# Modulation products of a two-block transformer kernel: summed along the row by GpSimd and VectorE instead of over partitions by TensorE

## What is computed

```python
s_c = jax.nn.silu(c)
s_cc = jax.nn.silu(c_ctx)[None]
...
ml = (s_c @ w_mod[i] + b_mod[i]).reshape(-1, 3, 3, D)
...
mc = (s_cc @ w_mod[i] + b_mod[i]).reshape(-1, 3, 3, D)
h = gated_residual(h, ml, 0, swiglu(ada_in(h, norm_g[i, 0], ml, 0), ffn_w_in[i, 0], ffn_w_out[i, 0]), 0.5)
```

## Time and profile before

| | |
|---|---|
| device time, median of 3 runs | 3246.8 us (3246.36 to 3249.54) |
| span of the profiled execution | 3230.1 us; no time of its own is shown for it beside the runs |
| PE busy | 3136.0 us (97% of the span) |
| PEld busy | 2660.2 us (82%) |
| DVE busy | 1724.8 us (53%) |
| ACT busy | 1270.9 us (39%) |
| POOL busy | 1950.4 us (60%), in 1285 instructions |
| DMA | 430.35 MB, mean 133 GB/s |

### The profile page before, as it was taken

One profiled execution on the slowest core, in us unless ns is written; L12 is line 12 of the kernel. 1 busy time (PEld: TensorE's weight loads), 2 busy tenths in 40 slices (PEclk: granted clock), 3 DMA queues, 4 the chain that ended last, 5 costly groups with the idle time before them and its releaser, 6 DMA issues.

```text
span 3230.1 us, 48616 instructions
## 1 busy us (share of the span) xinstructions
PE 3136.0 (97%) x18046; PEld 2660.2 (82%) x18046; DVE 1724.8 (53%) x2409; ACT 1270.9 (39%) x2132; POOL 1950.4 (60%) x1285
## 2 busy tenths in 40 slices
PE   7999899999999999999999999999999999999998
PEld 6677899976779998888887777888888888886898
DVE  5665776655668865443435465544435443436554
ACT  4445555343555643222232443322223222235443
POOL 6658477514994975677567658678875777603000
PEclk9999999999999999999999999999999999999999
DMA  5323455632335663333443223334433443332354
GB/s 195 111 92 105 138 189 194 204 105 95 112 117 168 215 210 121 122 126 122 134 130 117 85 85 108 119 129 130 136 125 110 133 138 125 123 119 76 131 182 156
DMA packets 120280, 430.35 MB, mean 133 GB/s; under 512 B 13857, under 2 KB 17185, under 8 KB 119729
## 3 DMA queue, kind: packets, MB, share of 16 engines
q1 hardware_dynamic: 93632, 335.24, 31.7%
q0 software_dynamic: 24576, 86.46, 8.4%
q10 hardware_dynamic: 1904, 6.36, 0.5%
HBM read 426.95 MB, written 8.85 MB: 135 GB/s over the span
## 4 chain that ended last, share of the span: by engine, by line
PE 86%; POOL 5%; DVE 3%; ACT 2%; DMA 2%; issue 2%; ACTq 0%; DVEq 0%; SPq 0%; POOLq 0%
PE ps L484 22%; PE ps L486 21%; PE ps L485 21%; PE ps L511 2%; PE ps L581 2%; PE ps L582 2%; PE ps L583 2%; POOL macc L402 2%; DMA raw<-in_panels 2%; POOL modraw L400 2%; POOL mprod L400 1%; PE ps L525 1%; PE ps L530 1%; PE ps L526 1%; PE ps L986 1%
## 5 line engine op out<-in xcount | busy, mean ns | idle before, releaser
L1642 DVE TENSOR_TENSOR wlo<-raw,whi 128x1024 fp32r<-128x1024 f32 x632 | 856.0, 1355 | 914.6 <-ACT whi L1078 889.5
L1078 ACT ACTIVATE whi<-raw 128x1024 fp32r<-128x1024 f32 x632 | 668.4, 1058 | 1417.2 <-PE ps L486 901.2
L484 PE MATMUL ps<-xhi,whi 128*128 128x512 f32 (+2 forms) x2792 | 949.3, 340 | 3.1 <-DVE wlo L1642 2.5
L486 PE MATMUL ps<-xhi,wlo 128*128 128x512 f32 (+2 forms) x2792 | 934.6, 335 | 0.0
L485 PE MATMUL ps<-xlo,whi 128*128 128x512 f32 (+2 forms) x2792 | 933.7, 334 | 0.0
L484 PEld LDWEIGHTS ps<-xhi,whi 128*128 128x128 f32 x2792 | 531.8, 190 | 70.8 <-issue 14.8
L485 PEld LDWEIGHTS ps<-xlo,whi 128*128 128x128 f32 x2792 | 531.8, 190 | 51.8 <-issue 1.9
L486 PEld LDWEIGHTS ps<-xhi,wlo 128*128 128x128 f32 x2792 | 531.4, 190 | 50.2
L400 POOL TENSOR_SCALAR modraw<-modraw,cs 128x512 f32<-128x512 f32 x288 | 552.1, 1917 | 27.6
L400 POOL TENSOR_SCALAR macc<-modraw,cs 128x512 f32<-128x512 f32 x36 | 70.5, 1958 | 745.2 <-PE ps L511 602.5
L400 POOL TENSOR_SCALAR mprod<-modraw,cs 128x512 f32<-128x512 f32 x252 | 445.8, 1769 | 19.0 <-POOL macc L402 0.2
(11 more groups left out here) (362 smaller groups left out, 4752.9 us busy)
## 6 DMA issues: line engine op xcount, KB each, us to landing
raw<-in_panels SPq DMA_DIRECT2D x632, 512.0 KB, 3.3
modraw<-in_mod POOLq DMA_DIRECT2D x144, 512.0 KB, 4.4
bias_by_column<-in_rpb POOLq DMA_DIRECT2D x16, 476.2 KB, 8.3
bia<-bias_by_column POOLq DMA_DIRECT2D x32, 96.0 KB, 2.6
rtab<-in_rtab ACTq DMA_DIRECT2D x2, 1312.0 KB, 7.4
wuq<-in_wuq ACTq DMA_DIRECT2D x2, 768.0 KB, 6.7
con<-in_con SPq DMA_DIRECT2D x1, 1345.5 KB, 13.7
h<-in_x SPq DMA_DIRECT2D x1, 1088.0 KB, 6.7
```

Source lines behind the costliest of these rows:

```text
L484: pe.matmul(out, w_hi, x_hi, start=start, stop=False)
L486: return pe.matmul(out, w_lo, x_hi, start=False, stop=stop)
L1078: act.activation(whi[:, s * PW:(s + 1) * PW], raw[:, s * PW:(s + 1) * PW], ACT.Copy).then_inc(hi_split, 1)
L1642: dve.tensor_tensor(wlo[:, s * PW:(s + 1) * PW], raw[:, s * PW:(s + 1) * PW], whi[:, s * PW:(s + 1) * PW].bitcast(F32), ALU.subtract).then ...
```

## The change

POOL now gets the weights turned: the 128 outputs of a tile lie on the partitions and the 1024 inputs along the row, in two pieces of 512 (`MOD_W`), 256 KB each. The conditions are loaded once by SP as a row that is repeated on all partitions (`cb`, 128 x 2048), and ACT applies the silu to all of it after the first norm, where before it did so to 16 columns inside that norm. For each piece POOL multiplies by both conditions and then halves the row again and again by adding its second half to its first, for both conditions in one instruction, down to 32 columns (`MOD_FOLD`), which go to `modacc`. A group has 4 tiles of 2 pieces and so 4 x (6 + 7) = 52 instructions, all `tensor_tensor`, and 8 loads. The wait for `mod_done` moves from the group's start to its first write of `modacc`, the sixth instruction. PE's 36 groups of matmuls go, with the PSUM bank they took. DVE's `mod_tiles` waits for POOL itself, sums `modacc` (128 x 8 x 32) to 128 x 8 with a `tensor_reduce`, and then adds the bias. In the five norms it stands at the end instead of behind the diagonals. The places of all other groups on DVE stay.

```diff
-MS = 30
+MOD_W, MOD_FOLD = 512, 32
+
+
+MOD_OPS = (6, 7)
+MS = 4 * sum(MOD_OPS)
...
+            sp.dma_start(cb[:, :], t["cond"].broadcast_to([P, 2 * D])).then_inc(cond_in, 16)
...
-                acc = [macc[:, s * 512:(s + 1) * 512] for s in range(2)]
-                for q in range(4):
-                    s = q % 2
-                    w = [modraw[:, s * PW + k * 512:s * PW + (k + 1) * 512] for k in range(2)]
...
-                    for k in range(2):
-                        if q or k:
-                            step(mprod[:, :], w[k], c[0][k], ALU.mult)
-                            step(acc[0], acc[0], mprod[:, :], ALU.add)
...
-                    for k in range(2):
-                        step(w[k], w[k], c[1][k], ALU.mult)
-                    if q:
-                        step(acc[1], acc[1], w[0], ALU.add)
-                        step(acc[1], acc[1], w[1], ALU.add)
...
+                if g in POOL_HOLD:
+                    pool.wait_ge(nlo_ready, POOL_HOLD[g])
+                for m in range(4):
+                    for s in range(2):
+                        prod, w = modraw[:, 0:MOD_W], mod_slot(s)
+                        both = modraw[:, :].rearrange("p (t n) -> p t n", t=3)[:, 0:s + 2:s + 1, :]
+                        acc = modacc[:, 2 * m * MOD_FOLD:2 * (m + 1) * MOD_FOLD].rearrange("p (t n) -> p t n", t=2)
+                        pool.wait_ge(mod_landed[s], 16 * (4 * g + m + 1))
+                        step(prod, w, cb[:, s * MOD_W:(s + 1) * MOD_W], ALU.mult)
+                        step(w, w, cb[:, D + s * MOD_W:D + (s + 1) * MOD_W], ALU.mult)
+                        n = MOD_W // 2
+                        while n > MOD_FOLD:
+                            step(both[:, :, 0:n], both[:, :, 0:n], both[:, :, n:2 * n], ALU.add)
+                            n //= 2
+                        if s == 0:
+                            if m == 0 and g:
+
+                                pool.wait_ge(mod_done, g)
+                            step(acc, both[:, :, 0:n], both[:, :, n:2 * n], ALU.add)
                         else:
+                            step(both[:, :, 0:n], both[:, :, 0:n], both[:, :, n:2 * n], ALU.add)
+                            step(acc, acc, both[:, :, 0:n], ALU.add)
+                        if m < 3 or not last:
+
+                            pool.wait_ge(mod_step, g * MS + steps)
+                            pool.dma_start(w, t["mod"][8 * g + 2 * m + s + 2, :, :]).then_inc(mod_landed[s], 16)
...
-            def mod_group():
-
-                b = new_bank()
-                lane.take(mod_step, MS)
-                for j in range(4):
-                    for s in range(2):
-                        o = (2 * j + s) * SUM_W
-                        last = pe.matmul(bank(b, o, o + SUM_W), macc[:, s * 512 + j * P:s * 512 + (j + 1) * P], ones[:, 0:SUM_W], start=True, stop=True)
-                last.then_inc(mod_done, 1)
...
-                if c == 0:
-                    act.wait_ge(const_in, 32)
-                    act.activation(cs[:, :], par[:, P_C:P_C + 2 * NC], ACT.Silu).then_inc(silu_c, 1)
...
                 norm(T1, between=first_chunks if layer == 0 else None)
+                if layer == 0:
+                    act.wait_ge(cond_in, 16)
+                    act.activation(cb[:, :], cb[:, :], ACT.Silu).then_inc(silu_c, 1)
...
                 inverse_roots(T)
-                if mod:
-                    mod_tiles()
...
                 low(NC - 1)
                 lane.take(nlo_ready, 2)
+                if mod:
+                    mod_tiles()
...
             def mod_tiles():
 
-                g, b = lane.count(mod_done).static, lane.tile.slot(BANKS)
-                lane.count(mod_done).add()
-                lane.tile.add()
-                dve.wait_ge(mod_done, g + 1)
+                g = lane.count(mod_done).static
+                dve.wait_ge(mod_step, (g + 1) * MS)
+                dve.tensor_reduce(modsum[:, :], modacc[:, :].rearrange("p (c n) -> p c n", n=MOD_FOLD), AX, ALU.add).then_inc(mod_done, 1)
+                lane.take(mod_done)
                 bm = par[:, P_BMOD + 4 * g:P_BMOD + 4 * g + 4].unsqueeze(2).broadcast_to([P, 4, 2])
-                dve.tensor_tensor(modv[:, 8 * g:8 * g + 8].rearrange("p (m s) -> p m s", s=2),
-                                  bank(b).rearrange("p (m s x) -> p m s x", s=2, x=SUM_W)[:, :, :, 0], bm, ALU.add).then_inc(bank_free[b], 1)
+                step(dve.tensor_tensor(modv[:, 8 * g:8 * g + 8].rearrange("p (m s) -> p m s", s=2), modsum[:, :].rearrange("p (m s) -> p m s", s=2), bm, ALU.add))
```

More of the change, by code:

```diff
@@ L69 @@
 P_C = DEPTH * PL
-P_BMOD = P_C + 2 * NC
+P_BMOD = P_C
 P_NG = P_BMOD + DEPTH * MODT
@@ L396, in step @@
                     nonlocal steps
-                    if steps or not (isinstance(g, int) and g == 0):
+                    if steps or g:
                         pool.wait_ge(mod_step, g * MS + steps)
-                    if op is ALU.mult:
-                        pool.tensor_scalar(out, a, b, None, op).then_inc(mod_step, 1)
-                    else:
-                        pool.tensor_tensor(out, a, b, op).then_inc(mod_step, 1)
+                    pool.tensor_tensor(out, a, b, op).then_inc(mod_step, 1)
@@ L538, in first_tiles, with tiles @@
                     walk(NC - 1, (j,)).then_inc(panel_done, 1)
-            def tiles(n, x_hi, x_lo, T, w, first=0, mod_at=(), middle=None):
-                for i, (_, count) in enumerate(parts(n, mod_at)):
-                    if i:
-                        mod_group()
-                    tiles_run(count, x_hi, x_lo, T, w, 0 if i else first, middle)
-            def tiles_run(n, x_hi, x_lo, T, w, first, middle):
+            def tiles(n, x_hi, x_lo, T, w, first=0, middle=None):
                 if first:
@@ L626, in fold_spread, with residual_tiles @@
                     pe.matmul(bank(5, c0, c0 + P), ones, rs[:, i * P:(i + 1) * P], start=True, stop=True).then_inc(rs_spread, 1)
-            def residual_tiles(K, x_hi, x_lo, T, w, norm=None, mod_after=(), ready=None, mod_norm=False):
+            def residual_tiles(K, x_hi, x_lo, T, w, norm=None, ready=None):
                 norm = T if norm is None else norm
@@ L1122, in root, with norm @@
                 act.activation(sm[:, 48:48 + n], bank(6, 0, n * SUM_W).rearrange("p (n x) -> p n x", x=SUM_W)[:, :, 0], ACT.Sqrt, bias=eps[:, 0:1], scale=1.0 / D).then_inc(root_done, 1)
-            def norm(T, shifts=None, then=None, between=None, mod=False):
+            def norm(T, shifts=None, then=None, between=None):
                 root(T)
-                lane.tile.add(mod)
                 if then:
@@ L1156, in residual @@
                         squares(m, norm_)
-                    lane.tile.add(2 if m in mod_after else 1)
+                    lane.tile.add()
                 if gain is not None:
@@ L1409, in _ @@
                 lane.count(part_lo).add(NC)
-                residual(NC, T, mod_after=MOD_OUT, gain=layer * PL + P_LN2)
+                residual(NC, T, gain=layer * PL + P_LN2)
                 def relu(i):
@@ L1435, in next_hidden @@
                     squared(i)
-                for i, (at, n) in enumerate(parts(FF1, MOD_TILES)):
-                    lane.tile.add(i > 0)
+                for at, n in parts(FF1, MOD_TILES):
                     panels(1, first_hidden, extra=((part_lo, 1),), first=at)
@@ L1442, in _ @@
                     act.wait_ge(ctx_in, 16)
-                residual(FF1, T, T1 if layer < DEPTH - 1 else T2, MOD_FF)
+                residual(FF1, T, T1 if layer < DEPTH - 1 else T2)
                 if layer + 1 < DEPTH:
@@ L1452, in shifts, with swiglu @@
                 return of
-            def swiglu(layer, j, T, norm_=None, mod=False, mod_after=()):
-                norm(T, shifts(layer, j, T), then=ACT.Silu, mod=mod)
+            def swiglu(layer, j, T):
+                norm(T, shifts(layer, j, T), then=ACT.Silu)
                 def pair(i):
@@ L1465, in pair @@
                     act.activation(col(ghi, i, T2, T), sq[:, (b // 2) * T2:(b // 2) * T2 + T], ACT.Copy).then_inc(part_hi, 1)
-                for part, (at, n) in enumerate(parts(2 * FF2, MOD_TILES2 if mod else ())):
-                    lane.tile.add(part > 0)
-                    with lane.loop(n // 4, [(lane.panel, 4), (lane.split, 4), (lane.tile, 4)]) as i:
-                        pair(i * 2 + at // 2)
-                        pair(i * 2 + (at // 2 + 1))
-                residual(FF2, T, norm_, mod_after)
+                with lane.loop(2 * FF2 // 4, [(lane.panel, 4), (lane.split, 4), (lane.tile, 4)]) as i:
+                    pair(i * 2)
+                    pair(i * 2 + 1)
+                residual(FF2, T)
             def block2():
                 lane.take(mod2_ready)
-                swiglu(0, 0, T2, None, True, MOD_FF2)
+                swiglu(0, 0, T2)
                 act.dma_start(rtab[:, :], t["rtab"]).then_inc(rtab_in, 16)
-                norm(T2, shifts(0, 1, T2), mod=True)
```

(1 more changed line is left out.)

96 lines of the change are left out of this document (32 added, 64 removed).

## The result

The changed kernel takes **3250.8 us** (median of 10 runs, 3244.93 to 3257.8) beside 3245.0 us for the kernel before (10 runs, 3233.28 to 3249.54): a ratio of 1.0034, 95% interval 1.0021 to 1.0047. It is 0.34% slower. The forecast was 3217.0 us, with 0.76 for faster and 0.16 for slower: the sign is wrong. (The time does lie inside the stated range of 3190 to 3255, near its upper end.)

The account below looks back on a forecast made before the run. PE was taken as the bound, busy 97% of the span. Of 55.4 us gained, 10 (groups 3 and 10), 8 (first feed-forward), 6 (DVE's splits) and 1 (start) were lost: 30 us gained, 3217 us, range 3190 to 3255.

Parts of the forecast that it names:

- What PE gives back: Removing PE's 36 matmul groups: 29 at 1.79 us each, five in norms at 0.7 us each; 55.4 us gained.
- the 1 us for the start: At the kernel's start, ACT's silu of 2048 columns and the load of `cb` were to cost 1 us.
- GpSimd's short steps: In POOL's folding, steps over 256, 128 and 64 columns were estimated at 0.72, 0.45 and 0.31 us.
- The rival in which GpSimd is the bound: Short POOL steps cost 0.25 us more each, making block-two groups 72 us against 65.4 available; 3280 us, chance 0.14.
- Groups 3 and 10: In the differential attention of both layers, late groups make PE wait 4.8 us longer for scaled scores; 10 us together lost.
- the forecast waits in the first feed-forward: Group 12 comes 9.6 us late, half counted as 5 us; groups 5 and 13 cost 3 us; sum 8 us.
- The late groups: DVE waiting for POOL's groups: 10 us lost at groups 3 and 10, 8 us at 5, 12 and 13.
- where DVE is on the chain (3% of it, about 100 us) I count 6 us: DVE's splits wait longer wherever POOL runs, mostly hidden behind PE; 6 us lost where DVE is on the chain.
- The clock: Sign that the forecast is wrong: a lower granted clock where PE now pauses.
- PE waiting for `wlo` by more than 20 us: Sign that the forecast is wrong: PE's waits for `wlo` exceed some 20 us in all.
- the port lock eats the gain: Every POOL step shuts DVE out at its upper bound, delaying groups and splits; about 0 gained, 3247 us, chance 0.14.
- The reading of the row at 1403.51: A split begun inside a POOL product took 1.31 us, so products with a value per partition don't lock DVE out.

Follow-up runs that it names:

- e3: Kernel before, with GpSimd's 16 products per group as two-input tensor_tensor of the weights with themselves (wrong vectors); 3292.9 us, ratio to before 1.0171.
- e1: Changed kernel with all 52 GpSimd steps of a group cut to 8 or 16 columns, so GpSimd is nearly idle; 3157.9 us, ratio to before 0.9751.
- e6: Changed kernel with a fifth place for partial sums in block one, so GpSimd may finish the next group's first tile early; 3237.4 us, ratio to before 0.9987.
- e7: Changed kernel with both the duration-matched one-input steps of e5 and the five places of e6; 3161.3 us, ratio to before 0.9765.
- e5: Changed kernel with each GpSimd step a one-input tensor_scalar of matched duration, modulation not computed; 3192.6 us, ratio to before 0.9856.
- e2: Kernel before with its 30 GpSimd steps per group cut to 8 columns, PE's 36 groups kept; 3218.8 us, ratio to before 0.9937.
- e10: Kernel of e6 with GpSimd held in the retention until DVE has rotated queries and keys; 3221.5 us, ratio to before 0.9940.
- e8: Kernel of e6 with GpSimd held in groups 4 and 11 until DVE has written the differential attention's normed outputs; 3252.6 us, ratio to before 1.0052.

## Why the prediction was wrong

By its own steps:

- **What PE gives back** (55.4 us): right, a little low; 60.9 us with GpSimd nearly idle in both kernels, beside 54.4 (with the 1 us for the start).
- **GpSimd's short steps** (0.72, 0.45 and 0.31 us by the line through two rows): right. The least for 64 columns is 0.316 us, for 512 1.260. The rival in which GpSimd is the bound needed 0.25 us more and was wrong; in block two DVE never waited for it.
- **Groups 3 and 10** (8.9 us late, PE 4.8 us later on its scores; 10 us together): right in mechanism, and DVE's lateness in size. DVE waited 8.2 and 10.2 us, and PE came to the scores at 322.92, forecast 322.4. Of the forecast waits in the first feed-forward, the one at group 13 was 6.1 us and the one at 12 only 0.2 (forecast 9.6). The late groups were put at 18 us; removing them gave 13.4 us beside the lock and 31.3 without it, so their price depends on the other cause.
- **"where DVE is on the chain (3% of it, about 100 us) I count 6 us"**: this is the step that failed. The lock cost 58 to 76 us in the changed kernel. Part of it was there before, but no more than the 23.6 us that GpSimd's whole work cost then, so the change added some 35 us at the least (58.2 - 23.6) where 6 were counted; e3 shows that turning the 16 products alone into two-input steps adds 50. The 6 us were a share of a share, with no row and no bound on either side. Three things are wrong in it. The chain of waits names DVE only where it already ends a wait; a stretched DVE makes new such places (PE waited 29.6 us for `wlo` instead of 7.2, and 25.2 for the scaled scores instead of 6.6). The splits of block one were looked at, and the chain of small instructions in the differential attention (0.74 us more for each) and the rotation in the retention weren't. And only DVE's instructions on two SBUF tensors were taken to be held, while the one-tensor `TENSOR_SCALAR` of the scaling is too.
- **The clock**: named as a sign that would prove the forecast wrong, and given no price. PE's busy time for the same matmuls is 28.6 us more than in e1. Two of the named signs came true: this one (0.89 instead of 0.93 from group 10 to 11) and PE waiting for `wlo` by more than 20 us.

The account closes by the medians: 60.9 gained, less 31.3 for late groups, 58.2 for the lock beside them and 3.4 unexplained, and 23.6 given back for what GpSimd had cost before, make -8.4 us, where the forecast had 30.

Of the rivals, *the port lock eats the gain* gave 3247 and a chance of 0.14; with 3250.8 it was nearly the number, and its cause is the main one. Its places were mostly wrong: it put 38 us on late groups (20 in the first feed-forward, 18 at groups 3 and 10), 10 on splits in the first feed-forward and 8 elsewhere. From e6 to e7 the stretches of the feed-forward, from group 4 to 6 and 11 to 13, did lose 11 us to the lock; but 38.7 us were lost from 3 to 4 and 10 to 11, and 11 in the retention, for which it had no term of its own. Its sentence against itself, that by the Trainium skill's rule at its word the products would have locked DVE out before too, is what e3 and e5 refute. The reading of the row at 1403.51, the split that wasn't held beside a GpSimd product, was right, and should have carried more weight: it meant that 25 us of harmless work per group turned into harmful work, 36 times.

Could a better size have been had beforehand? GpSimd's two-input time goes from 17.7 us per group to 43.4, by a factor of 2.4, and scaling the 23.6 us of e2 by it gives 57, about the 58 of e5. But this agreement is luck: in e3 the two-input time goes by the least durations from 17.7 to 34.3 us (16 products of 1.04 more), for which the same rule gives 22 us more, and 50 were measured. And the 23.6 us needed a run. What the rows did say is that the 6 us had nothing under them; a term that is open to tens of microseconds would have put the forecast's faster and slower much nearer to even.

## What to carry to other kernels

A GpSimd step is not free because GpSimd is idle: with two SBUF tensors as inputs it held VectorE back here, and small VectorE instructions that the critical engine waited for took 0.74 us more each. So price such work by where VectorE is latency-critical and not by its mean load, prefer forms with one tensor and a value per partition there, and make GpSimd pause over such stretches if the stretch after it has room (e10 gained 16 us by it over e6; e8 moved the work to where PE waits for VectorE too, and lost 15). When moving work off the bottleneck, replace the new work by an equally long harmless form (as e5 does), since shortening or lengthening it changes the lateness at the same time.

## What the runs showed that was not expected

- A GpSimd `tensor_scalar` and a GpSimd `tensor_tensor` of the same duration do very different things to VectorE: 1547 us busy against 1962 in the same program. With the first, VectorE is hardly held (1508 us with GpSimd nearly idle), while GpSimd's steps are still some 400 us longer in all than at their least durations.
- VectorE's `tensor_scalar` on one SBUF tensor, 128 x 144, went from 0.30 to 0.56 us on average beside two-input GpSimd work, and three in a row took 3.34 us instead of 0.71.
- Short GpSimd steps beside it: 0.32 us for 64 columns, 1.26 for 512 with two inputs; with one input 0.43 us for 56 columns and 0.81 for 206, so the one-input form isn't the faster one.
- PE's pauses cost more than they last: the 66.1 us more of idle time than in e1 came with 28.6 us more for the same matmuls, at a mean granted clock of 0.973 instead of 0.984.
- A GpSimd `tensor_tensor` over 512 columns that reads one tensor as both inputs (e3) took 1.04 us at the least, with two tensors 1.26.
